# Moving the pair sums of two token tiles from VectorE to ScalarE and GpSimd

## The reference

```python
def post_norm(i, slot, x, gate, out):
    return layer_norm(DEEPNORM_ALPHA * x + gate * out, ln_g[i, slot], ln_b[i, slot])

def channel_mixer(i, x, sh, sc, g):
    out = hier_moe(mod_in(x, sh, sc), w_rg[i], b_rg[i], w_re[i], b_re[i],
                   w_gate[i], w_up[i], w_down[i])
    return post_norm(i, 1, x, g, out)
```

## Time and profile before

| | us |
|---|---|
| median of three runs | 1438.0 |
| the profiled execution, own time | 1435.37 |
| its span, first to last instruction | 1433.2 |
| TensorE busy | 1091.2 (76%) |
| VectorE busy | 382.4 (27%) |
| ScalarE busy | 183.3 (13%) |
| GpSimd busy | 244.7 (17%) |
| mean granted TensorE clock | 0.897 of full speed |

### The profile page before, as it was taken

The page is one execution under the profiler, slowest core; times in us unless marked ns, Lnnn a source line. Parts: engine busy times, 40 slices in busy tenths (PEclk is TensorE's granted clock), DMA queues, the critical chain, the costliest instruction groups (busy, mean ns, idle before and its releaser), DMA issues.

```text
span 1433.2 us, 26875 instructions
## 1 busy us (share of the span) xinstructions
PE 1091.2 (76%) x9881; PEld 586.6 (41%) x9882; DVE 382.4 (27%) x917; ACT 183.3 (13%) x486; POOL 244.7 (17%) x446
## 2 busy tenths in 40 slices
PE   4899998697587777656648999999935757788781
PEld 1333345444244444323224444677433423444440
DVE  0120117767311111101043002322772101111117
ACT  0110026300000000000012001542000000000000
POOL 2000002200133333212112010000001212333330
PEclk9999997997599999978787999898957978999996
DMA  9866891118959999999975992101079999999932
GB/s 367 293 242 257 341 364 57 59 60 309 414 212 395 415 416 414 415 416 415 397 287 87 110 165 101 59 1 59 30 274 413 412 414 416 415 366 370 416 111 112
DMA packets 84900, 389.72 MB, mean 272 GB/s; under 512 B 17613, under 2 KB 18125, under 8 KB 56697
## 3 DMA queue, kind: packets, MB, share of 16 engines
q1 hardware_dynamic: 62624, 349.77, 63.0%
q0 software_dynamic: 15200, 36.74, 9.2%
q10 hardware_dynamic: 7032, 2.66, 0.7%
HBM read 379.65 MB, written 17.44 MB: 277 GB/s over the span
## 4 chain that ended last, share of the span: by engine, by line
DMA 40%; PE 35%; issue 10%; DVE 9%; ACT 2%; DVEq 1%; POOLq 1%; POOL 0%; SPq 0%; ACTq 0%; PEldq 0%
DMA ring<-in_w_down_dram 32%; PE ps L800 15%; PE ps L951 6%; DMA ybuf<-yo,idy 4%; PE ps L1040 4%; DMA ring<-in_w_ada_dram 2%; PE ps L1058 2%; PE ps L921 2%; PE ps L776 1%; PE ps L888 1%; DMA ring<-in_w_gate_dram 1%; PE ps L895 1%; POOLq L450 1%; PE ps L906 1%; DMA qkv<-ybuf 1%
## 5 line engine op out<-in xcount | busy, mean ns | idle before, releaser
L1040 PE MATMUL ps<-ring,xs 128*32 128x256 f32 x4928 | 311.1, 406 | 112.7 <-DMA ring<-in_w_up_dram 59.1
L1040 PEld LDWEIGHTS ps<-ring,xs 128*32 128x32 f32 x4928 | 183.8, 116 | 234.0 <-issue 126.2
L800 PE MATMUL ps<-ring,hT 128*128 128x512 f32 x576 | 256.3, 604 | 8.1 <-ACT hT L626 4.3
L1058 PE MATMUL ps<-ring,hm 128*32 128x256 f32 x2464 | 156.5, 394 | 32.0 <-ACT hm L734 26.0
L800 PEld LDWEIGHTS ps<-ring,hT 128*128 128x128 f32 x576 | 110.1, 193 | 153.4 <-issue 143.0
L1058 PEld LDWEIGHTS ps<-ring,hm 128*32 128x32 f32 x2464 | 72.8, 112 | 91.7 <-ACT hm L734 39.9
L1507 DVE COPY yo<-ps 128x256 f32<-128x256 f32 x73 | 31.0, 425 | 237.2 <-DMA ybuf<-yo,idy 179.6
L539 POOL DMA_INDIRECT xg<-xmod,idx x77 | 80.8, 1050 | 66.3 <-POOL idx L536 61.4
L731 ACT ACTIVATE sg<-ps 128x128 f32<-128x128 f32 x73 | 20.3, 278 | 560.0 <-PE ps L1040 553.2
L951 PE MATMUL ps<-ring,qT 128*128 128x512 f32 x192 | 84.7, 601 | 2.7 <-DVE qT L1309 1.6
L550 POOL DMA_INDIRECT ybuf<-yo,idy x73 | 75.1, 1029 | 64.4 <-POOL idy L547 62.6
(11 more groups left out here) (257 smaller groups left out, 853.0 us busy)
## 6 DMA issues: line engine op xcount, KB each, us to landing
ring<-in_w_gate_dram SPq DMA_DIRECT2D x82, 1024.0 KB
ring<-in_w_up_dram SPq DMA_DIRECT2D x82, 1024.0 KB
ring<-in_w_down_dram SPq DMA_DIRECT2D x82, 1024.0 KB
ring<-in_w_ada_dram SPq DMA_DIRECT2D x48, 1024.0 KB, 8.1
ring<-in_w_qkv_a_dram SPq DMA_DIRECT2D x12, 1024.0 KB, 5.2
ring<-in_w_qkv_b_dram SPq DMA_DIRECT2D x12, 1024.0 KB, 15.4
modb<-mdram POOLq DMA_DIRECT2D x12, 512.0 KB, 7.1
qkv<-ybuf SPq DMA_DIRECT2D x6, 1024.0 KB, 8.3
```

The lines of the kernel that those rows point to most:

```text
L800: ins = mm(ps[:, 2 * t + hf, :], lhs[:, k, t * P:(t + 1) * P], raw[:, slot, kk * D + hf * 512:kk * D + (hf + 1) * 512], start=(k == 0), st ...
L1040: ins = mm(ps[j * BLK:(j + 1) * BLK, 1, 0:W].rearrange("p (a n) -> p a n", a=2), xs[:, k, :], w[:, :, at:at + FW], start=(k == 0), stop=(k ...
L1058: ins = mm(ps[j * BLK:(j + 1) * BLK, 5, 0:WD], hm[:, 2 * c + q, :], ring[:, slot + GU + c, q * D + j * WD:q * D + (j + 1) * WD], start=(c ...
```

## The change

For tiles 1 and 2, in both layers:

- ScalarE gets a second instruction: it multiplies the second expert's output by its gate weight in place, `ypair[:, 2t+1, :] *= w1`, ahead of the one that it had.
- GpSimd gets two instructions with two tensor inputs each, 128x1024: it adds the scaled halves in `ysum`, and multiplies the sum by the modulation row. The second raises a new semaphore, `y_mix`.
- VectorE waits for `y_mix` and does only `x = ALPHA * x + ysum`, the sums and the mean and variance. Its two instructions ahead of that are gone.

Tile 0 stays on VectorE as before; only its product is written to `ysum` rather than to `t1`. In sum, per layer, VectorE has four 128x1024 instructions fewer, ScalarE two more, GpSimd four more.

```diff
--- before.py
+++ after.py
@@ -248,7 +248,7 @@
         sq_done, sq_rdy, hn_rdy = sem("sq_done"), sem("sq_rdy"), sem("hn_rdy")
         yg_ld = [[sem(f"yg_ld{l}_{t}") for t in range(NT)] for l in range(LAYERS)]
         x_rdy, y_half, nmr_rdy = sem2("x_rdy"), sem2("y_half"), sem("nmr_rdy")
-        h_last, y_out = sem("h_last"), sem("y_out")
+        h_last, y_out, y_mix = sem("h_last"), sem("y_out"), sem("y_mix")
 
 
 
@@ -567,6 +567,11 @@
 
                 if l == 0:
                     load_affine(l, 1)
+                pool.wait_ge(lnb_ld, 64 * (2 * l + 1) + 32)
+                for t in range(1, NT):
+                    pool.wait_ge(y_half[l], t + 1)
+                    chain(pool.tensor_tensor(ysum[:, t, :], ysum[:, t, :], ypair[:, 2 * t + 1, :], ALU.add))
+                    pool.tensor_tensor(ysum[:, t, :], ysum[:, t, :], modb[:, 1, :], ALU.mult).then_inc(y_mix, 1)
                 wait_apart(pool, pool_steps, gath[l], n_blk * 16 + 32)
                 wait_apart(pool, pool_steps, y_wr[l], n_blk * 16)
                 if l == 0:
@@ -743,6 +748,8 @@
 
                 for t in range(NT):
                     act.wait_ge(yg_ld[l][t], 16)
+                    if t:
+                        act.activation(ypair[:, 2 * t + 1, :], ypair[:, 2 * t + 1, :], ACT.Copy, scale=gatew[:, 1, t:t + 1])
                     act.activation(ysum[:, t, :], ypair[:, 2 * t, :], ACT.Copy, scale=gatew[:, 0, t:t + 1]).then_inc(y_half[l], 1)
                 if l == 0:
 
@@ -1176,12 +1183,14 @@
             def take_experts(l, t):
 
                 dve.wait_ge(y_half[l], t + 1)
-                chain(v.scalar_tensor_tensor(ysum[:, t, :], ypair[:, 2 * t + 1, :], gatew[:, 1, t:t + 1], ysum[:, t, :],
-                                             ALU.mult, ALU.add))
                 if t == 0:
+                    chain(v.scalar_tensor_tensor(ysum[:, t, :], ypair[:, 2 * t + 1, :], gatew[:, 1, t:t + 1], ysum[:, t, :],
+                                                 ALU.mult, ALU.add))
                     dve.wait_ge(lnb_ld, 64 * (2 * l + 1) + 32)
-                chain(v.tensor_tensor(t1[:, :], ysum[:, t, :], modb[:, 0 if t == 0 else 1, :], ALU.mult))
-                chain(v.scalar_tensor_tensor(x[:, t, :], x[:, t, :], ALPHA, t1[:, :], ALU.mult, ALU.add))
+                    chain(v.tensor_tensor(ysum[:, t, :], ysum[:, t, :], modb[:, 0, :], ALU.mult))
+                else:
+                    dve.wait_ge(y_mix, (NT - 1) * l + t)
+                chain(v.scalar_tensor_tensor(x[:, t, :], x[:, t, :], ALPHA, ysum[:, t, :], ALU.mult, ALU.add))
                 for i in range(2):
                     v.bn_stats(st[:, i, :], x[:, t, i * 512:(i + 1) * 512])
                 dve.drain()
```

## The result

The changed kernel is slower. Its median over four runs is 1452.51 us (1451.74 to 1453.18), beside 1439.07 us for the kernel before in four runs (1436.76 to 1441.94): 13.4 us more, which is a ratio of 1.0093. The ratio on record, 1.0102 with a 95% interval of 1.0086 to 1.0119, would be 14.7 us. I had forecast 1439.6 us, no change that a measurement can tell, with 1443.5 as the upper end. The profiled execution has a span of 1449.7 us against 1433.2.

A forecast was written before the change was run, and what follows sets the result against it. Gapless VectorE work was taken to bound layer 1's end, a chain of VectorE, ScalarE and TensorE layer 0's. Terms of +0.47 and +1.12 made +1.6 us on the median 1438.0: 1439.6 us, range 1433.5 to 1443.5.

The forecast's parts named there:

- The sum with the hold: Both layers' ends, GpSimd and VectorE holding each other: +0.47 us in layer 1, +1.12 in layer 0, together +1.6.
- the third rival: Head of each end: GpSimd's code is fetched anew, 4.94 us ahead of the first pair; about +11.5, 1449.5 us; chance 0.05.
- What goes: VectorE in each end: tile 2 loses two instructions, 2.66 us; tile 1 loses 2.67; tile 0 keeps its three.
- ScalarE at no cost: ScalarE in the ends: a second 128x1024 activation per tile, 2.37 us for two in a row, costs nothing by itself.
- GpSimd's 2.34 us: GpSimd in the ends: each two-input 128x1024 operation takes 2.34 us, the middle of 1.27, 2.34 and 3.40.
- The hold in both directions: VectorE and GpSimd in the ends: whichever two-input operation is in flight blocks the other engine's until it is done.
- The first rival: Both ends: only GpSimd is held, VectorE is not; sum -3.6 us, 1434.4 us; chance 0.28.
- Who goes first at the release of tile 1: Start of tile 1's `x` in each end: VectorE first, holding GpSimd; otherwise line 1121 comes out within 0.2 us.
- The fourth rival: Both ends: GpSimd is quick, 1.27 us an operation; layer 1 -3.7 us, layer 0 -3.0, 1431.3 us; chance 0.03.
- the second: Both ends: held both ways with longer GpSimd operations; +2.9 us from 2.50 on, about +10 at 3.40; chance 0.19.
- The price of 8 times each 0.1 us of length: Four GpSimd operations ahead of line 1121 in each end: 0.1 us of operation length is 0.8 us in the sum.

The follow-up runs named there:

- e1_warm: The changed kernel plus one drained 128x4 GpSimd addition behind each expert stage's last scatter: 1437.85 us, ratio 1.0009 to the kernel before.
- e2_scalar_only: The kernel before with only ScalarE's scaling for tiles 1 and 2 and a plain addition on VectorE: 1437.82 us, ratio 1.0002.
- e6_timed: The kernel before plus a small drained GpSimd addition and tile 2's addition on GpSimd, started after VectorE's tile 1 `x`: 1434.2 us, ratio 0.9987.
- e4_tile2: The changed kernel plus the small drained GpSimd addition, with tile 1 back on VectorE and only tile 2 moved: 1440.87 us, ratio 1.0031 to the kernel before.

## Why the prediction was wrong

The step that failed is the head of each end in "The sum with the hold". There GpSimd's second operation follows the first by 0.15 us, so the sum has nothing for a wait in the drain between them. It stood only as the third rival, "the code of the operations has to be fetched anew", with a chance of 0.05. I had its row (222.74, 4.94 us of idle time) and its place, and held against it that within that stage it came once. But the row says only that additions which follow additions don't wait; it says nothing of additions behind a stage of gathers and scatters. No row of before had an addition there, so nothing stood against the rival. It did have the price elsewhere, and I did not look there: GpSimd's closing drain, 7.50 us behind layer 1's stage. The runs put the term at 7.28 and 7.60 us, and e1_warm, where it is covered, is not told from before.

By the rival's own sum (+1.6 for the rest and one wait in each end) the measured waits give +16.5; the profile shows +16.5 and the medians +13.4. That the first two agree to a tenth is luck: the ends carry 15.4 of it, and the rest of the change came out at +0.9, not +1.6. I had 1449.5 with the shorter wait. I had also looked for the gap before the first operation; it came behind it. The rival's name is not borne out either: a drain with no operation ahead of it waits as long, so no missing code of the additions is needed to explain the gap. What the drain waits for stays open.

The other steps, in their order:

- What goes: I had 2.66 us for tile 2. In the changed kernel's layer 1 the instruction on `x` of tile 2 follows the `finish` before it by 0.18 us (1438.17 to 1438.35) where it was 2.76 (1419.02 to 1421.78), so 2.58.
- ScalarE at no cost: right (e2_scalar_only, 1.0002).
- GpSimd's 2.34 us: right. It was the middle of three cases worked out from VectorE's pace and GpSimd's fixed share; that it is right to the digit is in part luck. The estimate from the Trainium skill, GPSIMD Engine Reference, section 3.1, half of 4497 ns, was 2.25; the trace says 2.34.
- The hold in both directions: right. A two-input VectorE instruction takes 3.26 instead of 1.23 behind a GpSimd operation in flight. The Trainium skill, SBUF — State Buffer, section "SBUF: two separate sides", has the rule that the one which starts first keeps the shared ports to its end; the trace agrees. The first rival (VectorE not held, 1434.4) falls.
- Who goes first at the release of tile 1: I had VectorE, it was GpSimd, 0.16 earlier (752.08 and 752.24), because no drain stands between its second operation and its third, where I had put 0.15. So the long hold fell on VectorE's instruction on `x` (2.03 us) and not on the root, where one small operation was held by 0.33, and of GpSimd's operations the fourth was stretched (0.79) and not the third (I had 1.2). I had said that the root would come out within 0.2 of the same; by e1_warm it came 0.3 earlier.
- The sum with the hold, +1.6: +0.9 by the trace of e1_warm and +0.5 by its medians (ratio 1.0009, interval 0.9997 to 1.0020). In layer 1 the root is 2.79 us late and tile 2 gives back 2.58, so the two terms nearly cancel, as forecast.
- The fourth rival, GpSimd at 1.27 us, and the second, over 2.50, both fall with the measured 2.34.
- The price of 8 times each 0.1 us of length was not put to the test, since the length was right.

## What to carry to other kernels

An engine that is idle is not free: ask what its first instruction of a kind costs at that place, drains included. If no row shows one there, an earlier row with such a gap is a term of the sum and not a rival with a small chance; and look among the instructions that do not count as busy, where the drain of 7.50 us stood. Here a small addition with its drain, put where the engine waited anyway, covered the gap. A drain alone should do the same; no run tried it. GpSimd's two-input work beside VectorE's two-input work was no parallel work here: each held the other. Beside VectorE's sums and mean it ran freely, but the gain of that (e6_timed) was not told from none. TensorE, idle in the same ends, was the better place: its diagonal matmuls took 5 us off the ends where GpSimd's additions had paid nothing.

## What the runs showed of the hardware

- GpSimd's first drain behind an expert stage took 7.50 us with no arithmetic operation ahead of it (closing drain in layer 1). As idle time behind a first operation the wait was 5.9 to 8.5 us there (5.9, 6.0 and 8.5 with narrow operations, 7.3 and 7.6 with wide ones), 4.9 in layer 0's attention of the kernel before, and 5.9 and 7.8 ahead of a stage. In layer 1 of the changed kernel no engine worked and no DMA packet moved meanwhile.
- The Trainium skill, GPSIMD Engine Reference, section 2.1, tells of about 6 us at the first call to a freshly loaded kernel. The trace's 7.3 to 7.6 came at operations of a kind that had run before, 470 us and more earlier; the changed kernel's two MODIFY_POOL_CONFIG instructions stand at 201.2 us, and the closing drain waited with no such call at all.
- What GpSimd held on VectorE was not only two-input instructions: a one-input operation of 128x2 took 0.50 and 0.80 us instead of 0.17, ending within 0.03 us of GpSimd's end, while the sums (`bn_stats`, 1.29 for two) and the mean ran beside it at full pace.
- Two engines that hold each other alternated one instruction each (e4_tile2): every instruction then took about the rest of the other's and its own time (VectorE 3.20 us, GpSimd 2.86 and 3.14).
